# Every second up projection by seven block products in a one-core hybrid decoder step

## The reference, cut to what matters

```
h2 = rms_norm(x, norm_mlp) * (1.0 + sc_m) + sh_m
x = x + g_m * (jnp.square(jax.nn.relu(h2 @ w_up)) @ w_down)     # w_up 1024 x 4096, w_down 4096 x 1024
```

## Time and profile before

| | before |
|---|---|
| median of 3 runs | 1150.89 us (1148.16 to 1153.05) |
| the profiled execution | 1151.07 us, its span 1149.3 us |
| TensorE busy | 1103.8 us, 96% |
| VectorE busy | 683.2 us, 59% |
| ScalarE busy | 487.1 us, 42% |
| GpSimd busy | 88.0 us, 8% |
| mean granted clock | 0.983 |

### The profile page before, as it was taken

The page is one execution under the profiler, slowest core; times in us unless marked ns, Lnnn a source line. Parts: engine busy times, 40 slices in busy tenths (PEclk is TensorE's granted clock), DMA queues, the critical chain, the costliest instruction groups (busy, mean ns, idle before and its releaser), DMA issues.

```text
span 1149.3 us, 21500 instructions
## 1 busy us (share of the span) xinstructions
PE 1103.8 (96%) x8725; PEld 1044.2 (91%) x8725; DVE 683.2 (59%) x1512; ACT 487.1 (42%) x851; POOL 88.0 (8%) x65
## 2 busy tenths in 40 slices
PE   5999999998999999999999999899999999999997
PEld 4798889977899999999899998899999999999997
DVE  5735654545487877778876456537455553636475
ACT  3544556466544454643444225442323223332334
POOL 2400000000000000000000012320101001010101
PEclk9899999998999999999999999899999999999998
DMA  9884423212332413222232471222232223223202
GB/s 303 273 305 147 131 91 112 74 38 74 119 93 61 121 49 109 77 76 74 77 107 65 171 240 37 74 74 75 74 111 74 74 84 101 74 74 110 73 3 83
DMA packets 108775, 120.20 MB, mean 105 GB/s; under 512 B 2692, under 2 KB 98780, under 8 KB 108389
## 3 DMA queue, kind: packets, MB, share of 16 engines
q1 hardware_dynamic: 108677, 118.83, 31.9%
HBM read 108.99 MB, written 11.80 MB: 105 GB/s over the span
## 4 chain that ended last, share of the span: by engine, by line
PE 79%; DVE 12%; ACT 5%; issue 3%; DMA 1%; POOL 0%; SPq 0%; DVEq 0%; ACTq 0%; POOLq 0%
PE PS L849 59%; PE PS L802 4%; PE PS L958 3%; DVE wR L1405 2%; DVE xhat L1373 1%; PE PS L822 1%; ACT wR L1088 1%; PE PS L793 1%; PE PS L928 1%; PE PS L906 1%; PE PS L892 1%; DMA xn<-in_x_sample 1%; ACT pr L1215 1%; PE PS L769 1%; PE PS L998 1%
## 5 line engine op out<-in xcount | busy, mean ns | idle before, releaser
L849 PE MATMUL PS<-hR,wR 128*128 128x288 f32 x3744 | 524.8, 298 | 0.8 <-issue 0.8
L849 PEld LDWEIGHTS PS<-hR,wR 128*128 128x128 f32 x3744 | 504.0, 189 | 9.8 <-issue 8.9
L1405 DVE TENSOR_TENSOR wR<-raw,wR 128x512 fp32r<-128x512 f32 x260 | 203.1, 781 | 108.0 <-ACT wR L1088 100.6
L849 PE MATMUL PS<-actR,wR 128*128 128x288 f32 (+2 forms) x1920 | 259.3, 296 | 1.8 <-DVE actR L1547 1.8
L849 PEld LDWEIGHTS PS<-actR,wR 128*128 128x128 f32 x1920 | 255.5, 188 | 3.0 <-DVE actR L1547 2.0
L1088 ACT ACTIVATE wR<-raw 128x512 fp32r<-128x512 f32 x260 | 164.4, 632 | 142.4 <-PE PS L849 132.9
L1467 DVE CAST actR<-tmp 128x576 fp32r<-128x576 f32 x32 | 15.2, 476 | 128.4 <-ACT tmp L1199 128.4
L802 PE MATMUL PS<-wR,hR 128*128 128x256 f32 x600 | 77.5, 286 | 0.0
L802 PEld LDWEIGHTS PS<-wR,hR 128*128 128x128 f32 x600 | 73.4, 191 | 1.8 <-issue 1.7
L1198 ACT ACTIVATE tmp<-PS 128x576 f32<-128x576 f32 x32 | 20.8, 651 | 122.7 <-PE PS L849 119.6
L1422 DVE SCALAR_TENSOR_TENSOR xT<-PS,mods,xT 128x288 f32<-128x288 f32 x68 | 35.2, 518 | 61.2 <-PE PS L849 54.9
(11 more groups left out here) (219 smaller groups left out, 1071.8 us busy)
## 6 DMA issues: line engine op xcount, KB each, us to landing
raw<-in_w_in SPq DMA_DIRECT2D x30, 1024.0 KB, 5.2
raw<-in_w_up SPq DMA_DIRECT2D x16, 1024.0 KB, 5.4
raw<-in_w_down SPq DMA_DIRECT2D x16, 1024.0 KB, 5.0
mid<-in_w_ada SPq DMA_DIRECT2D x12, 1024.0 KB, 5.2
ada<-in_w_ada SPq DMA_DIRECT2D x8, 1024.0 KB, 12.1
S<-in_state_hgrn SPq DMA_DIRECT2D x8, 512.0 KB, 4.6
out_hgrn_sample<-S SPq DMA_DIRECT2D x8, 512.0 KB, 6.7
raw<-in_w_out SPq DMA_DIRECT2D x4, 1024.0 KB, 5.7
```

What stands on the lines that cost most here:

```text
L849: mm = pe.matmul(PS[:, 2 * x.pair + h, 0:size], weights(x, w, k, col), rhs[r], start=(k == 0 and n == 0), stop=(k == last and n == 2))
L1405: done(dve.tensor_tensor(w[:, 1, cols], raw[SLOT[SPLITS[n]]][:, cols], w[:, 0, cols].bitcast(F32), ALU.subtract), s_lo)
```

## The change

Up units 3, 5, 7, ..., 15 (`SEVEN`, seven units) are cut into 2 x 2 blocks: weights by column tile and half of k (`cut`: first digit the column tile, second the half of k), tokens by half of k and token half (`tokens_of`). The four output blocks come from seven block products, with sums of blocks on both sides: S1 = w21 + w22, S2 = S1 - w11, S3 = w11 - w21, S4 = w12 - S2, and T1 = t12 - t11, T2 = t22 - T1, T3 = t22 - t12, T4 = t21 - T2. A product is 4 k x 3 terms = 12 matmuls.

- TensorE runs `product` seven times (banks 7, 5 and 6; bank 7 is accumulated over products 0, 2, 4 and 6, and ScalarE copies it out between them).
- VectorE makes the sums of weight blocks (`sums`, 4 of 128x512 a unit) before the copies and subtractions, which are seven pieces instead of four (`PIECES`), spread over the chunks of the plain up unit before.
- The token sums T1 to T4 are made once in up 1 (`combine`, 128x1152), and split into high and low parts in up 1, 2 and 3 (`halve`: a ScalarE copy and a VectorE subtraction of 128x1152 each). They read the modulated activations in fp32, so `modulate` of the MLP leaves these in `xhat1` and not in four turning buffers, and two waits for GpSimd (`s_hlo`) go away there.
- ScalarE copies four product results out of PSUM (128x288), VectorE adds three (`seven`); relu, square and the rounded copy are ScalarE's, the low part VectorE's, half of it in the following down unit (`relu`, `squares_of`, `low`).
- In the down unit behind a seven-product unit the split of the next unit begins two chunks later (`LAST_SEVEN`: behind the first residual).
- In plain up units the low part is made by VectorE, directly behind its cast. GpSimd has no part in evacuations any more.
- `levels`, the masks of the recurrence, move into a staged region; the new buffers lie over `late` and `xhat1`.

```diff
+SEVEN = [u for u, x in enumerate(UNITS) if x[0] == "up" and x[1] >= 3 and x[1] % 2]
+PRODUCTS = [("11", "11", 0, True), ("12", "21", 1, True), ("S2", "T2", 0, False), ("S1", "T1", 2, True),
+            ("S3", "T3", 0, False), ("S4", "22", 2, False), ("22", "T4", 0, False)]
+PIECES = ["11", "12", "S1", "S3", "S2", "22", "S4"]
+MIXED = [("T1", "12", "11"), ("T2", "22", "T1"), ("T4", "21", "T2"), ("T3", "22", "12")]
+HALVED = [(1, 5), (1, 7), (2, 7), (3, 3)]
+LAST_SEVEN = {u + 1: u for u in SEVEN if u + 1 < len(UNITS) and UNITS[u + 1][0] == "dn"}
...
             at = x.n * parts(x) + c if x.half != 1 else 4
-            if at < 4 and (x.kind, x.i) != ("up", 0) and x.split + 1 < len(SPLITS):
+            if LAST_SEVEN.get(x.u) is not None:
+                at -= 2
+            if (x.kind, x.i) != ("up", 0) and x.split + 1 < len(SPLITS) and 0 <= at < CUTS[x.split + 1]:
...
+            def product(x, c):
+                j = SEVEN.index(x.u)
+                wa, tb, i, start = PRODUCTS[c]
+                bank = bank_of(x, i)
+                pe.wait_ge(s_lo, cuts(x.split, PIECES.index(wa) + 1))
...
+                elif c == 1:
+                    if j:
+                        pe.wait_ge(s_added, 3 * j - 2)
+                elif c == 3:
+                    if j:
+                        pe.wait_ge(s_added, 3 * j)
+                else:
+                    pe.wait_ge(s_kept, 4 * j + {2: 1, 4: 2, 5: 3, 6: 4}[c])
+                for k in range(4):
...
+                    for n, (l, r) in enumerate(((0, 0), (0, 1), (1, 0))):
+                        mm = pe.matmul(bank[:, 0:HALF], w[l], t[r], start=(start and k == 0 and n == 0), stop=(k == 3 and n == 2), skip_group_check=True)
...
+            def seven(x, c):            # ScalarE
...
+                if c == 5:
+                    act.wait_ge(s_added, 3 * j + 3)
+                    done(act.activation(kept(x, 0)[:], kept(x, 0)[:], ACT.Relu))
+                    squares_of(x, 0)
+                    return
...
+                done(act.activation(halves_of(x, dst[0])[dst[1]], bank[:, 0:HALF], ACT.Copy), s_kept)
...
                 for k in (k0, k0 + 1):
-                    if k >= 4:
+                    if k >= 4 and n == 0:
                         dve.wait_ge(s_hlo, n * KT + k - 3)
...
+            def sums(n, q):             # VectorE
...
+                if q == 0:
+                    dve.wait_ge(s_raw[SLOT[u]], raw_loads(u))
+                    done(dve.tensor_tensor(one, cut(w, "21"), cut(w, "22"), ALU.add), s_sum)
+                    done(dve.tensor_tensor(three, cut(w, "11"), cut(w, "21"), ALU.subtract), s_sum)
+                elif q == 3:
+                    done(dve.tensor_tensor(one, one, cut(w, "11"), ALU.subtract), s_sum)
+                elif q == 5:
+                    done(dve.tensor_tensor(one, cut(w, "12"), one, ALU.subtract), s_sum)
...
-                    dve.wait_ge(s_sq2, n + 1)
-                    done(dve.tensor_copy(actR[:, act_tile(x), 0, :], tmp[n % 2][:]), s_ahi)
+                    dve.wait_ge(s_sq2, PLAIN.index(x.t) + 1)
+                    a_ = actR[:, act_tile(x)]
+                    done(dve.tensor_copy(a_[:, 0, :], tmp[x.n][:]))
+                    done(dve.tensor_tensor(a_[:, 1, :], tmp[x.n][:], a_[:, 0, :].bitcast(F32), ALU.subtract), s_alo)
...
-            def evac(x):
-                if x.kind == "up":
-                    n = 2 * x.i + x.n
-                    pool.wait_ge(s_ahi, n + 1)
-                    a_ = actR[:, act_tile(x)]
-                    done(pool.tensor_tensor(a_[:, 1, :], tmp[n % 2][:], a_[:, 0, :].bitcast(F32), ALU.subtract), s_alo)
```

More of the change, by code:

```diff
@@ L153, in tiles @@
             out.append(Tile(len(out), u, kind, i, n, split, 6 + i % 2))
+        elif u in SEVEN:
+            out.append(Tile(len(out), u, kind, i, n, split, 8 + n))
         else:
@@ L167, with cuts @@
 ADDED = [(x.half, k) for x, k in zip(FINAL, FINAL_K) if 0 < k <= SUMMED]
+def cuts(n, q=0):
+    return sum(CUTS[:n]) + q
+PLAIN = [x.t for x in TILES if x.kind == "up" and x.u not in SEVEN]
 TANH = [x.t for x in TILES if x.kind in ("rq", "ga", "gr", "rg")]
@@ L176, in count_read @@
         return TANH.index(t) + 1
-    return sum(READER[x.kind] == reader for x in TILES[:t + 1])
+    return sum(READER[x.kind] == reader and x.u not in SEVEN for x in TILES[:t + 1])
 PREP = 4
@@ L315, in walk @@
                 yield ("mm", x, c)
+            at_ = x.n * parts(x) + c
+            if squared is not None and at_ == 0:
+                yield ("low", squared, 0)
+            elif squared is not None and at_ == 2:
+                yield ("low", squared, 1)
+                squared = None
             if guest and c == 1:
@@ L332, in walk @@
                     yield ("load", AFTER[SPLITS[x.split + 1]])
+            if x.kind == "up" and (x.i, at_) in HALVED:
+                yield ("halve", HALVED.index((x.i, at_)))
+            if x.u in SEVEN:
+                yield ("seven", x, c)
+            if squared is not None and at_ == 0:
+                yield ("relu", squared)
+            elif squared is not None and at_ == 1:
+                yield ("squared", squared)
             if merging and c in (0, 2):
@@ L436, in stage @@
             st, out = ExitStack(), []
-            for name, shape in tensors:
-                out.append(sb(name, shape, F32, st))
+            for name, shape, *dt in tensors:
+                out.append(sb(name, shape, *(dt or [F32]), st))
             st.close()
@@ L1684, in _ @@
                     merge(*x)
+                elif ev == "combine":
+                    combine(*x)
+                elif ev == "halve":
+                    halve(*x)
+                elif ev == "seven":
+                    seven(*x)
+                elif ev == "low":
+                    low(*x)
                 elif ev == "y_put":
```

190 lines of the change are left out of this document (170 added, 20 removed).

## The result

| | before | changed |
|---|---|---|
| median, first comparison | 1149.81 us (4 runs) | 1136.73 us (4 runs, 1133.97 to 1139.33) |
| ratio | | 0.9885 (0.9859 to 0.9910) |
| median, second comparison | 1148.72 us (9 runs) | 1135.79 us (4 runs) |
| ratio | | 0.9883 (0.9862 to 0.9905) |
| profiled execution | 1151.07 us | 1136.93 us (span 1135.0) |

The direction was right, and so was the main mechanism (fewer matmuls in a stage that they bound); a second gain, which the sum did not have, came on top.

What follows compares the result with a forecast made beforehand. TensorE's matmuls were taken to bound the kernel from 742 to 1117 us; 11.13 us removed less 0.3 for up 3 gave 10.8, so 1150.89 - 10.8 = 1140.1 us, range 1137.0 to 1146.0.

Steps and rivals of the forecast that it cites:

- VectorE's and ScalarE's load: Per round in the stage from 742 us: VectorE busy 32.8 us of 49.4, ScalarE 20.7 us.
- the copies' slack: In seven-product units, ScalarE's copy of a product's bank ends 1.08 us before TensorE needs that bank.
- product waits cost nothing by themselves: Up to 2 new TensorE waits before each of 49 products: between 0 and 6.0 us, taken as 0.
- VectorE's own low part is no burden: In up tiles, VectorE's low part costs 0.76 us, replacing GpSimd's, which blocked VectorE for 1.27 us.
- the joint unit: The joint first up unit, paced by a small VectorE operation held by GpSimd; change costed at 0.
- The 132.3 ns from the window: Matmul pitch from a 51.00 us window said to hold 385.5 matmuls; fences by tile gave 132.5, which was used.
- Removed: Seven seven-product units behind 742 us drop 84 matmuls at 132.5 ns each, saving 11.13 us.
- The 0.3 us for up 3: In up 3, a halving delays ScalarE's copy of product 3 before product 5: cost 0 to 1 us, taken 0.3.
- the range's working: Range's upper end: a 0.85 us TensorE idle once a unit, 7 x 0.85 = 6.0 us, would give 1145.9 us.
- Exposed weight loads: Rival: each of 49 products begins with an exposed weight load, 9.2 us, giving 1149.3 us; chance 0.07.
- VectorE and ScalarE holding each other up: Rival: last S pieces late in each seven-product unit, 7 x 0.75 = 5.3 us lost, giving 1145.4 us; chance 0.09.
- Pauses with a falling clock: Rival: TensorE idles 14% of each seven-product unit, clock 0.79, 4.6 us a unit, giving 1172 us; chance 0.05.

Runs made afterwards that it cites:

- the first experiment: Kernel before with only the up tiles' low parts moved from GpSimd to VectorE, no block products: 1148.50 us, ratio 0.9994.
- either part of the change alone: Kernel before with only VectorE's low parts (1148.50 us, 0.9994), or only the next split starting two chunks later in down units behind two up units (1148.35 us, 0.9986).
- the units in turn: Changed kernel with units ordered up, down, up, down, still seven seven-product units: 1147.94 us, ratio 0.9982.
- three needless copies: Changed kernel with three needless ScalarE copies of 256 columns before each of the four copies of a product's bank: 1162.76 us, ratio 1.0113.
- thirteen units: Changed kernel with all up units from 3 on by seven products, order up, down, up, down, next split one chunk late: 1142.04 us, ratio 0.9928.
- the order mended: Thirteen units with first two sums at the down unit's start, pieces two chunks late, seventh piece behind the next product 0: 1129.06 us, ratio 0.9829.

## Why the prediction was nearly right, and what was wrong in it

**Right.** The stage is bound by the matmul count; a seven-product unit costs its 84 matmuls; VectorE's and ScalarE's load; the copies' slack; that product waits cost nothing by themselves (11.15 against 11.13 us); that VectorE's own low part is no burden (in the first experiment VectorE is busy 27.3 us of a round, against 26.8: nearly paid for by the blocking that goes); that the joint unit is not changed (709.48 to 733.08 = 23.60 us before, 708.16 to 731.75 = 23.59 in the changed kernel's first profile).

**The step that failed** is the one ahead of the sum: "so from 742 to 1117 us each matmul that is gone is worth its pitch", taken as the whole of the stage. I read the pitch from the smooth stretches, and the absence of stalls from a wait list that can't show short ones. The fences of a whole round, 51.05 us, against 384 x 132.5 = 50.88 were in the trace and unread. The 132.3 ns from the window was a misreading besides: the row counts 385 matmuls, not 385.5, and a count in a window is off by one or two. The change removes this stall as a side effect, up to 7 x 0.17 = 1.2 us, so the term "Removed", put at 11.13 us, measured 12.0 to 12.1 net. What removed it was shown from both sides: either part of the change alone brings the round of the kernel before to 50.88, and the changed kernel keeps 49.32 with GpSimd's low parts back.

**Sizes.** The 0.3 us for up 3 didn't occur in the changed kernel's first profile (up 3 takes 11.15 there); in its second profile one wait stands there, at product 2 and not at product 5, and the unit takes 756.60 to 768.35 = 11.75:

```profile
760.28 1.83 PE L898 MATMUL PS<-tR,wx_S 128*128 128x288 f32 x12 [0.37 <-ACT kept L1262]
```

A larger part of the miss is the base: I subtracted from 1150.89, the median of three runs; with the fourth run of the first comparison it is 1149.81, and the 29 runs of before in one later comparison have 1149.32. So of the 3.4 us between 1140.1 and 1136.73 about 1.0 is the stall, 0.3 the cost that did not occur, 1.1 the base of that comparison, and 1.0 is left, within scatter: the ratio's interval is a gain of 10.3 to 16.2 us, which holds the forecast 10.8 as well as the 12.0. The time alone would not have shown the stall; the round does. That the median fell below 1137.0 is in part chance: 1149.3 - 12.1 is 1137.2, just inside the range. (In the range's working, 1140.1 and 6.0 make 1146.1, not 1145.9.) Of the 14.3 us between the two profiled spans, 1.3 were there before the joint unit, 12.0 came between up 1's start and the last down tile (733.08 to 1108.46 against 731.75 to 1095.11), 0.9 behind; what the 1.3 and the 0.9 come from is not shown.

**What I had underrated** is a part costed at nothing. I described the two chunks' delay as a detail of ScalarE's order; without it 1.70 us of each round's 1.73 are gone. Had I asked what an edit costs if its cover is gone, the shortest cover in the stage would have been in the prediction: there are 3.18 us between a down tile's end and the need for its bank, the residual takes 1.26 of them to free it, and some 0.2 go for signals (my estimate, from the 0.2 us between a tile's end and ScalarE's start). That leaves about 1.7 us of lateness for everything that stands ahead of the residual; the kernel before used all of it.

**The rivals.** Exposed weight loads: refuted (11.15 us a unit). VectorE and ScalarE holding each other up: not in this kernel, but it is the real danger of this change, as the runs without the delay and with the units in turn show. Pauses with a falling clock: refuted for the pauses of 0.4 to 0.6 us a product that three needless copies make.

## What to carry to other kernels

When TensorE bounds a stage, measure the period of the repeating round between two fences and subtract the matmuls times their pitch; what is left is a stall, whatever the busy share says. Before adding work to an engine that frees banks, list for each bank the time between a tile's end and the need for it; order, not load, decides in these runs: at about 65% busy VectorE cost nothing or 1.7 us a round, at 77% (thirteen units) 0.87 us a unit, and at 79% with the order mended nothing again. Put new work where the engine idles ahead of a wait, not where its data happen to be ready.

## What the hardware showed that I had not expected

- The same program starts up 1 in two ways. The last 16 matmuls of the joint unit take 4.21 us in the changed kernel's first profile and 2.36 in its second (4.21 or 2.38 to 2.40 in those of the other kernels), and up 1 and 2 together 27.39 or 25.52 us. The windows over the start of up 1, of the changed kernel's first and second profile, differ in the granted clock (0.73 and 1.00):

```profile
731.00:740.00 9.00, 8.25 (x48) 8.28 (x49) 7.02 (x9) 5.20 (x8) 0.00 (x0) 0.73 0.36 113
```

```profile
731.00:740.00 9.00, 8.93 (x67) 8.96 (x68) 7.59 (x10) 5.90 (x9) 0.00 (x0) 1.00 0.38 119
```

  Pauses of up to 1.9 us stand ahead of it in both. By these numbers some 3.7 us of the scatter between runs can come from here; why one execution falls to 1.2 GHz and another doesn't was not settled.
- With TensorE idle for 14% of a unit in four pauses of 0.4 to 0.6 us, its granted clock stayed at 1.00 (three needless copies).
- A subtraction over strided blocks of 128 columns takes 0.69 us (0.691 to 0.693 over the seven units), the same as a contiguous one.
